# Two latent heads scored in one step of the even layer's attention, and a third tile behind its projections

## Chip, cores and metric

The kernel runs on 1 core of one Trainium2 chip. The metric is the device time of one execution in microseconds (us). The median of the runs of a kernel is what is compared.

## What is computed

A two-layer block runs first (feed-forward, a mixer of three branches, cross attention, feed-forward), then a second two-layer block on two streams of 256 rows each, x and a context. The change lies in layer 0 of that second block, its "even" mixer, which has four differential heads and four latent heads. For the latent heads (`mla_attend` in the reference) the part that matters is

```python
def mla_attend(qn, qr, kn, kr, v):
    s = (jnp.einsum('bhqd,bhkd->bhqk', qn, kn) + jnp.einsum('bhqd,bkd->bhqk', qr, kr)) * ((MLA_NOPE + MLA_ROPE) ** -0.5)
    p = softmax_f32(s)
    return jnp.einsum('bhqk,bhkd->bhqd', p.astype(v.dtype), v)
```

`qn`, `kn` have 128 numbers a head, `qr`, `kr` have 64; `kr` is shared by the heads. A differential head takes two softmaxes over keys of 64 numbers each and subtracts them. The context attends to its own 256 keys, x to 512 keys (the context's and its own). Everything is float32; the large weight products are split in three products of a faster type, the attention's products are plain float32.

## The kernel before

One Python program is run five times, once for each engine, and only that engine's instructions are emitted. Waits are counted semaphores, so the order on each engine is the order in which the program emits.

**Two streams woven by hand.** `second` starts two generators, `rows` (stream x) and `context`, and `weave` (L420) interleaves them. Each `yield` hands back an estimate in us of the TensorE work just emitted: about 2.8 for a block of weights of 256 x 512, 1.39 and 2.09 for the blocks of the two small projections out of the latent, 1.8 for a group of the modulation, 0 or a negative number where a stream has to wait for a latency. Rows go first, and the context goes first once it has earned 2.7 us (0.6 of what rows emitted). A stream that yields 0 or less is passed over until other work has been emitted. Where neither can go, `weave` emits a group of the modulation (`co.mods`, eight small products on a plain 512 KB block of `mod_w`). After each turn `tick` (L347) advances all jobs in flight by one step.

**Projections.** `Even` (L2258) has `latent_gemm`, `dv_gemm`, `dk_gemm`, `dq_gemm` and, for c = 0 and 1, `kv_gemm` and `q_gemm`. All but `dv_gemm` copy their result out of the banks into a tile `etk` taken from a ring (`Turns`, L679) and spawn a job: squares, sums, a power on GpSimd, the scaling (`group_norm`, L2182), for x also the rotation (`rope`, L2231), then the transposes into `kv` or `q` (`t32`, `two_halves`), and only then `turns.give`. `when_free` (L449) holds back the last block of the next projection while the next tile of the ring is taken. The ring has two tiles. A job needs some five ticks for the context and five to nine for x. `Even.ready` lets attention start when the last job is done. The context's feed-forward also stops after 16 blocks until x's projections are ready.

**Attention.** `Even.attend` (L2438) goes over 16 items (t, h), two tiles of 128 rows by eight heads; h < 4 are the differential heads, h >= 4 the latent heads. In step i it emits: the products with the values for item i - 3, the transposes of the probabilities of item i - 2 and their copy on ScalarE, then the scores of item i (one bank for each softmax), the maximum on VectorE and the exponential on ScalarE, and for a differential item i - 1 the combination of its two softmaxes. Then it yields 0, and `hops` turns that into a pause of 4 for x and of 0 for the context, so that at least one block of the other stream (2.8 us, in the context's attention sometimes a half block of 1.4) lies between two steps. The score products of a differential head take the rows 0 to 63 and 64 to 127 of the operands, one after the other; those of a latent head are one over 128 rows (L2507) and one over 64 rows (L2509), where even heads use rows 0 to 63 and odd heads rows 64 to 127.

**Banks.** `next_bank` hands out the PSUM bank of eight that was used longest ago; `hold` keeps a bank until `let_go`.

**Weights.** A ring of five raw slots is filled by SyncE in the order of use, three blocks ahead (`stage`, L465). ScalarE rounds a block (`whi`) and VectorE forms the rest (`wlo`). A slot is loaded again when both are done, or, for a plain block of the modulation, when TensorE has used it.

Of the kernel before, what the change touches and what calls it, by code (L numbers as in the profile page):

```python
# [13 lines left out]
P = 128  # L14
# [282 lines left out]
def next_bank(co, hold=False):  # L297

    b = min((b for b in co.banks if not b.held), key=lambda b: b.since)
    co.bi += 1  # L300
    b.held, b.since = hold, co.bi
    return b


def let_go(co, b):
    co.bi += 1
    b.held, b.since = False, co.bi
# [1071 lines left out]
def columns_of(co, dst, banks, tok, scale, *after):  # L1379
    a, b = (v.ap.rearrange("p (k n) -> p k n", k=2) for v in banks)  # L1380
    co.ac.wait_ge(tok, after)
    banks[0].drained = co.ac.activation(dst[:, 0:2, :], a, ACT.Copy, scale=scale).then_inc(co.s_ac)
    co.dv.wait_ge(tok, after)
    banks[1].drained = co.dv.tensor_scalar(dst[:, 2:4, :], b, scale, None, ALU.mult).then_inc(co.s_dv)
    return (banks[0].drained, banks[1].drained)
# [545 lines left out]
class Memory:  # L1931
# [13 lines left out]
    def keys(self):  # L1945
        def evac(banks, tok):
            self.dep["k"] = columns_of(self.co, self.k, banks, tok, 1.0, self.fe)
        return gemm_t(self.co, (self.mh, self.ml), self.mdep, self.co.A["xa_wkv"][self.l], 0, 512, evac)
# [309 lines left out]
class Even:  # L2258
# [179 lines left out]
    def attend(self, s, room, pr, at_, sm, mx, fe, done):  # L2438


        co, dep, lam = self.co, self.dep, self.co.lam
        dqt, qnt, qrt = self.q
        nk = 512 if s == 0 else 256
        ns = nk // P
        streams = (1, 0) if s == 0 else (1,)
        y = room.tile
        keys = lambda r, at: self.kv[r, 0:len(streams), at:at + 256]
        have = lambda names, ss: tuple(v for k, v in dep.items() if isinstance(k, tuple) and k[0] in names and k[1] in ss)
        kdep, qdep = have(("dk", "dv", "kn", "kr", "mv"), streams), have(("dq", "qn", "qr"), (s,))
        R = len(pr)  # L2450
        pfree, afree, smfree = [fe] * R, [fe] * 2, [fe] * R
        items = [(t, h) for t in range(2) for h in range(8)]
        n = len(items)
        yb, st, norms = {}, {}, []

        def normed_heads(t, b, a):
            done.append((yield from group_norm(co, [b], y, [(0, 4, P)], a, (t,))))

        for i in range(n + 3):
            if i >= 3:  # L2460
                t, h = items[i - 3]
                q = (i - 1) % 2
                if h % 4 == 0:
                    yb[h // 4] = next_bank(co, hold=True)
                b = yb[h // 4]
                v = [(self.dv if h < 4 else self.mv)[r][:, i, :] for r in streams for i in range(2)]
                hh = h % 4
                co.pe.wait_ge(st[i - 3], b.drained)
                for k in range(ns):
                    m = co.pe.matmul(b.ap[:, hh * P:(hh + 1) * P], at_[q][:, k, :], v[k][:, hh * P:(hh + 1) * P], start=k == 0, stop=k == ns - 1, skip_group_check=True).then_inc(co.s_pe, k == ns - 1)  # L2470
                afree[q] = m
                if h == 3:
                    co.ac.wait_ge(m, room.free)
                    a = co.ac.activation(y[:, t, 0:512], b.ap, ACT.Copy).then_inc(co.s_ac)
                    norms.append(normed_heads(t, b, a))
                if h == 7:
                    co.dv.wait_ge(m)
                    a = co.dv.reciprocal(sm[:, t, :], sm[:, t, :]).then_inc(co.s_dv)
                    co.dv.wait_ge(a, room.free)
                    b.drained = a = co.dv.tensor_tensor(y[:, t, 512:1024].rearrange("p (g n) -> p g n", n=P), b.ap.rearrange("p (g n) -> p g n", n=P), sm[:, t, :].unsqueeze(2).to_broadcast([P, 4, P]), ALU.mult).then_inc(co.s_dv)  # L2480
                    let_go(co, b)
                    done.append(a)
            if 2 <= i < n + 2:
                r, q = (i - 2) % R, i % 2
                p, es = pr[r], st[i - 2]
                b = next_bank(co)
                co.pe.wait_ge(es, b.drained)
                for k in range(ns):
                    m = co.pe.transpose(b.ap[:, k * P:(k + 1) * P], p[:, 0, k * P:(k + 1) * P], ident(co, p[:, 0, k * P:(k + 1) * P])).then_inc(co.s_pe, k == ns - 1)
                pfree[r] = m  # L2490
                smfree[r] = (m, es)
                co.ac.wait_ge(m, afree[q])
                b.drained = co.ac.activation(at_[q][:, 0:ns, :], b.ap[:, 0:nk].rearrange("p (k n) -> p k n", n=P), ACT.Copy).then_inc(co.s_ac)
                st[i - 2] = b.drained
            if i < n:
                t, h = items[i]
                ts_ = slice(t * P, (t + 1) * P)
                r = i % R
                p, es, scores = pr[r], [], []
                sc = 64 ** -0.5 if h < 4 else 192 ** -0.5  # L2500
                for j in range(2 if h < 4 else 1):
                    b = next_bank(co)
                    co.pe.wait_ge(kdep, qdep, b.drained)
                    if h < 4:
                        m = co.pe.matmul(b.ap[:, 0:nk], dqt[64 * j:64 * j + 64, h, ts_], keys(slice(64 * j, 64 * j + 64), 256 * h), skip_group_check=True, start=True, stop=True).then_inc(co.s_pe)
                    else:
                        co.pe.matmul(b.ap[:, 0:nk], qnt[:, h - 4, ts_], keys(slice(0, P), 1024 + 256 * (h - 4)), stop=False, skip_group_check=True, start=True)  # L2507
                        rr = slice(64 * (h % 2), 64 * (h % 2) + 64)
                        m = co.pe.matmul(b.ap[:, 0:nk], qrt[rr, (h - 4) // 2, ts_], keys(rr, 4096), start=False, skip_group_check=True, stop=True).then_inc(co.s_pe)  # L2509
                    scores.append((b, m))  # L2510
                for j, (b, m) in enumerate(scores):
                    co.dv.wait_ge(m, smfree[r])
                    a = co.dv.tensor_reduce(mx[:, r, j:j + 1], b.ap[:, 0:nk], AX, ALU.max).then_inc(co.s_dv)
                    co.dv.wait_ge(a)
                    a = co.dv.tensor_scalar(mx[:, r, j:j + 1], mx[:, r, j:j + 1], -sc, None, ALU.mult).then_inc(co.s_dv)
                    acc = sm[:, t, h - 4:h - 3] if h >= 4 else mx[:, r, 2 + j:3 + j]
                    co.ac.wait_ge(a, pfree[r])
                    b.drained = co.ac.activation(p[:, j, 0:nk], b.ap[:, 0:nk], ACT.Exp, scale=sc, bias=mx[:, r, j:j + 1], accum_out=acc).then_inc(co.s_ac)
                    es.append(b.drained)
                st[i] = tuple(es)  # L2520
            if 1 <= i < n + 1 and items[i - 1][1] < 4:
                r = (i - 1) % R
                p = pr[r]
                co.dv.wait_ge(st[i - 1])
                a = co.dv.reciprocal(mx[:, r, 2:4], mx[:, r, 2:4]).then_inc(co.s_dv)
                co.dv.wait_ge(a, co.gains)
                a = co.dv.tensor_scalar(mx[:, r, 3:4], mx[:, r, 3:4], lam[:, 2:3], None, ALU.mult).then_inc(co.s_dv)
                b = co.dv.tensor_scalar(p[:, 0, 0:nk], p[:, 0, 0:nk], mx[:, r, 2:3], None, ALU.mult).then_inc(co.s_dv)
                co.dv.wait_ge(a, b)
                st[i - 1] = co.dv.scalar_tensor_tensor(p[:, 0, 0:nk], p[:, 1, 0:nk], mx[:, r, 3:4], p[:, 0, 0:nk], ALU.mult, ALU.add).then_inc(co.s_dv)  # L2530
            norms = [g for g in norms if next(g, StopIteration) is not StopIteration]
            yield 0
        while norms:
            norms = [g for g in norms if next(g, StopIteration) is not StopIteration]
            yield 0
# [358 lines left out]
def second(co, start):  # L2894
    A = co.A
    at = lambda off, name, shape, dt=F32: place(co, start + 1024 * off, name, shape, dt)
# [4 lines left out]
    for a, b in zip(co.ch, old):  # L2901
# [4 lines left out]
    co.stream = {1: Stream(tile, [ready, ready], small(C_SM, C_SM + 4, 2), counts(co))}  # L2906
    co.sm, co.mx = small(C_SM + 4, C_SM + 12, 2), small(C_SM + 12, C_SM + 28, 4)
    co.smo, co.mxo = small(C_SM + 28, C_SM + 60, 2), small(C_SM + 60, C_SM + 68, 4)
    ev = Even(co, at(16, "kv", [P, 2, 4352]), at(50, "q", [P, 2560]), [at(60 + 4 * i, "etk", [P, 2, 512]) for i in range(2)],
              (at(68, "cqh", [P, 2, 256], F32R), at(70, "cql", [P, 2, 256], F32R)),  # L2910
              (at(72, "ckh", [P, 1, 256], F32R), at(73, "ckl", [P, 1, 256], F32R)),
              at(74, "ew", [P, 2, 512]), co.lb[:, :].rearrange("p (t n) -> p t n", t=2))
# [94 lines left out]
```

## Time and profile before

| | |
|---|---|
| median of 3 runs | 2571.64 us (2565.17 to 2572.57) |
| the profiled execution | 2567.47 us, span 2565.7 us |
| TensorE busy | 2487.4 us, 97% of the span |
| VectorE, ScalarE busy | 1661.2 us (65%), 1275.6 us (50%) |
| the second block | from about 1290 us to the end |
| context's projections and attention | about 1321 to 1464 us, and 1466 to 1538 us |
| x's projections and attention | about 1586 to 1699 us, and 1700 to 1822 us |

Engines are PE (TensorE), PEld (its weight loads, which overlap), DVE (VectorE), ACT (ScalarE), POOL (GpSimd), SP (SyncE). A line such as L175 is that of a helper, so the tile names tell which operation it is: `kv,q` are scores, `cst,pc` and `cst,px` the transposes of the context's and x's probabilities, `kv,atc` and `kv,atx` the products with the values, `cst,etk` the transposes of the projections, `raw,cst` the modulation.

### The profile page before, as it was taken

How to read it: one execution, taken by the hardware profiler on the slowest of the kernel's cores; microseconds unless marked ns; L12 is line 12 of the kernel's file. 1: busy time of each engine (PE TensorE's matmuls, PEld its weight loads, DVE VectorE, ACT ScalarE, POOL GpSimd, SP SyncE). 2: the span in 40 equal slices, each digit the busy share in tenths (PEclk: the TensorE clock that was granted, in tenths of full speed). 3: DMA queues.
4: the chain of work that ended last, by engine and by line, in shares of the span. 5: the costliest groups of instructions: out<-in, count | busy, mean ns of one | idle time of the engine just before them, and what ended most of it. 6: DMA issues, size and time to landing. Idle time of an engine off the chain costs nothing. (4 is left out here: it accounts for less than half of the span.)

```text
span 2565.7 us, 40494 instructions
## 1 busy us (share of the span) xinstructions
PE 2487.4 (97%) x16401; PEld 2151.3 (84%) x16401; DVE 1661.2 (65%) x2442; ACT 1275.6 (50%) x1844; POOL 197.0 (8%) x260
## 2 busy tenths in 40 slices
PE   8999999999999999999999998999999999998999
PEld 8998877889989988788888886878897887665998
DVE  5556785775576576867765767776655655766555
ACT  4445545544444445444454564655453544554543
POOL 1000000011021000001010201200000001100000
PEclk9999999999999999999999999999999999999999
DMA  8755565768577564557566535553556558635564
GB/s 276 251 180 161 145 190 178 255 203 298 158 220 247 164 206 129 172 166 259 193 193 183 165 99 177 160 173 99 164 177 226 197 189 220 193 114 195 166 192 137
DMA packets 239371, 479.14 MB, mean 187 GB/s; under 512 B 17584, under 2 KB 38328, under 8 KB 239120
## 3 DMA queue, kind: packets, MB, share of 16 engines
q1 hardware_dynamic: 222288, 421.19, 52.0%
q0 software_dynamic: 16896, 55.37, 6.8%
q8 instruction: 129, 2.11, 0.3%
q14 instruction: 58, 0.48, 0.1%
HBM read 475.33 MB, written 6.92 MB: 188 GB/s over the span
## 5 line engine op out<-in xcount | busy, mean ns | idle before, releaser
L126 DVE TENSOR_TENSOR wlo<-raw,whi 128x1024 fp32r<-128x1024 f32 (+3 forms) x786 | 912.9, 1173 | 661.3 <-ACT whi L167 660.0
L167 ACT ACTIVATE whi<-raw 128x1024 fp32r<-128x1024 f32 (+3 forms) x786 | 789.3, 1017 | 609.6 <-PE bank L175 516.4
L175 PE MATMUL bank<-xh,whi 128*128 128x256 f32 x2208 | 627.9, 284 | 3.6 <-DVE xl L126 2.5
L175 PE MATMUL bank<-xl,whi 128*128 128x256 f32 x2208 | 621.4, 281 | 0.0
L175 PE MATMUL bank<-xh,wlo 128*128 128x256 f32 x2208 | 621.3, 281 | 0.0
L175 PEld LDWEIGHTS bank<-xh,whi 128*128 128x128 f32 x2208 | 417.9, 189 | 16.3 <-issue 8.7
L175 PEld LDWEIGHTS bank<-xl,whi 128*128 128x128 f32 x2208 | 417.9, 189 | 1.2 <-issue 0.5
L175 PEld LDWEIGHTS bank<-xh,wlo 128*128 128x128 f32 x2208 | 417.7, 189 | 0.0
L175 PE MATMUL bank<-whi,xh 128*128 128x512 f32 (+2 forms) x632 | 256.7, 406 | 8.8 <-DVE xl L126 3.8
L175 PE MATMUL bank<-whi,xl 128*128 128x512 f32 (+2 forms) x632 | 247.8, 392 | 0.0
L175 PE MATMUL bank<-wlo,xh 128*128 128x512 f32 (+2 forms) x632 | 247.1, 391 | 0.0
L175 PE MATMUL bank<-whi,uh 128*128 128x512 f32 x528 | 211.1, 400 | 0.2 <-DVE ul L126 0.2
L175 PE MATMUL bank<-wlo,uh 128*128 128x512 f32 x528 | 209.4, 397 | 0.0
L175 PE MATMUL bank<-whi,ul 128*128 128x512 f32 x528 | 209.2, 396 | 0.0
L175 PEld LDWEIGHTS bank<-whi,xh 128*128 128x128 f32 x632 | 120.3, 190 | 48.0 <-DVE wlo L126 15.1
L175 PEld LDWEIGHTS bank<-whi,xl 128*128 128x128 f32 x632 | 119.9, 190 | 27.1
L175 PEld LDWEIGHTS bank<-wlo,xh 128*128 128x128 f32 x632 | 120.4, 191 | 25.5 <-issue 1.4
L126 POOL TENSOR_TENSOR cst<-cst 128x8 f32<-128x8 f32 (+4 forms) x50 | 74.9, 1511 | 679.0 <-DVE cst L133 679.0
L175 PEld LDWEIGHTS bank<-whi,uh 128*128 128x128 f32 x528 | 99.7, 189 | 24.5 <-issue 1.4
L175 PEld LDWEIGHTS bank<-whi,ul 128*128 128x128 f32 x528 | 99.5, 188 | 24.1
L175 PEld LDWEIGHTS bank<-wlo,uh 128*128 128x128 f32 x528 | 99.6, 189 | 22.5
L175 PE MATMUL bank<-x2h,whi 128*128 128x256 f32 x352 | 100.4, 285 | 1.4 <-DVE wlo L126 1.4
(440 smaller groups left out, 3752.5 us busy)
## 6 DMA issues: line engine op xcount, KB each, us to landing
raw<-in_ffn_w_in SPq DMA_DIRECT2D x280, 512.0 KB, 4.4
raw<-in_ffn_w_out SPq DMA_DIRECT2D x154, 512.0 KB, 4.7
raw<-in_w_mix_in SPq DMA_DIRECT2D x112, 512.0 KB, 3.6
raw<-in_mod_w SPq DMA_DIRECT2D x50, 512.0 KB, 4.3
store<-in_mod_w POOLq DMA_DIRECT2D x46, 512.0 KB, 8.1
raw<-in_od_w_in SPq DMA_DIRECT2D x40, 512.0 KB, 4.7
raw<-in_ffn_w_in SPq DMA_DIRECT2D x56, 256.0 KB, 2.8
raw<-in_w_branch SPq DMA_DIRECT2D x24, 512.0 KB, 3.4
```

The lines of the kernel that those rows point to most:

```text
L126: return Made(self.e and self.e.tensor_tensor(out, a, b, op))
L167: return Made(self.e and self.e.activation(out, a, f, **k))
L175: return Made(self.e and self.e.matmul(out, lhs, rhs, **k))
```

## The change

In `attend` the scores of a latent head are no longer emitted in its own step. At an even latent head two banks are held and four products are emitted: the two over 128 rows of this head and the next, then the two over 64 rows, one on rows 0 to 63 and the other on rows 64 to 127. The step of the odd head emits no scores; its maximum and exponential are emitted there as before, on the bank that waited. Each bank is let go after its exponential. And the ring of `etk` gets a third tile, placed at an offset of 94 KB beside the two at 60 and 64 KB.

```diff
-                for j in range(2 if h < 4 else 1):
-                    b = next_bank(co)
-                    co.pe.wait_ge(kdep, qdep, b.drained)
-                    if h < 4:
+                if h < 4:
+                    for j in range(2):
+                        b = next_bank(co)
+                        co.pe.wait_ge(kdep, qdep, b.drained)
                         m = co.pe.matmul(b.ap[:, 0:nk], dqt[64 * j:64 * j + 64, h, ts_], keys(slice(64 * j, 64 * j + 64), 256 * h), skip_group_check=True, start=True, stop=True).then_inc(co.s_pe)
-                    else:
-                        co.pe.matmul(b.ap[:, 0:nk], qnt[:, h - 4, ts_], keys(slice(0, P), 1024 + 256 * (h - 4)), stop=False, skip_group_check=True, start=True)
-                        rr = slice(64 * (h % 2), 64 * (h % 2) + 64)
+                        scores.append((b, m))
+                elif h % 2 == 0:
+                    two = [next_bank(co, hold=True) for _ in range(2)]
+                    for j, b in enumerate(two):
+                        co.pe.wait_ge(kdep, qdep, b.drained)
+                        co.pe.matmul(b.ap[:, 0:nk], qnt[:, h - 4 + j, ts_], keys(slice(0, P), 1024 + 256 * (h - 4 + j)), stop=False, skip_group_check=True, start=True)
+                    both = []
+                    for j, b in enumerate(two):
+                        rr = slice(64 * j, 64 * j + 64)
                         m = co.pe.matmul(b.ap[:, 0:nk], qrt[rr, (h - 4) // 2, ts_], keys(rr, 4096), start=False, skip_group_check=True, stop=True).then_inc(co.s_pe)
-                    scores.append((b, m))
+                        both.append((b, m))
+                    scores.append(both[0])
+                else:
+                    scores.append(both[1])
...
                     es.append(b.drained)
+                    if h >= 4:
+                        let_go(co, b)
...
-    ev = Even(co, at(16, "kv", [P, 2, 4352]), at(50, "q", [P, 2560]), [at(60 + 4 * i, "etk", [P, 2, 512]) for i in range(2)],
+    ev = Even(co, at(16, "kv", [P, 2, 4352]), at(50, "q", [P, 2560]), [at(o, "etk", [P, 2, 512]) for o in (60, 64, 94)],
```

## Rows read from the trace of the kernel before

**Rows 1.** The page: busy time of the engines, TensorE's granted clock in 40 slices
```profile
PE 2487.4 (97%) x16401; PEld 2151.3 (84%) x16401; DVE 1661.2 (65%) x2442; ACT 1275.6 (50%) x1844; POOL 197.0 (8%) x260
...
PEclk9999999999999999999999999999999999999999
```
**Rows 2.** Stretches, all engines: the two attentions, and 30 us later on
```profile
core 0: us, PE busy (x) PEld busy (x) DVE busy (x) ACT busy (x) POOL busy (x), PEclk, DMA share, GB/s
1466.00:1545.00 79.00, 75.40 (x510) 62.49 (x510) 52.69 (x122) 46.15 (x99) 2.01 (x2) 1.00 0.37 112
1700.00:1822.00 122.00, 120.25 (x754) 95.04 (x753) 76.93 (x133) 66.79 (x108) 2.04 (x2) 1.00 0.39 122
1955.00:1985.00 30.00, 24.79 (x163) 19.80 (x162) 15.29 (x19) 11.22 (x14) 1.38 (x2) 0.91 0.66 238
```
**Rows 3.** Timeline, x's attention, a latent head (start us, length us, instruction)
```profile
1742.38 0.30 PEld L175 LDWEIGHTS bank<-kv,q 128*128 128x128 f32 x2
1743.44 0.30 PEld L175 LDWEIGHTS bank<-kv,q 64*128 64x128 f32 x2 [0.76 <-issue]
1744.50 0.19 PEld L175 LDWEIGHTS bank<-ch,whi 128*128 128x128 f32 x1 [0.76 <-issue]
```
**Rows 4.** The same, a differential head and what follows it
```profile
1755.13 1.13 PE L175 MATMUL bank<-kv,q 64*128 64x512 f32 x4
1756.19 0.39 PE L175 MATMUL bank<-ch,whi 128*128 128x256 f32 x1
```
**Rows 5.** Timeline, context's attention: a differential head, a latent head, each with its follower
```profile
1466.60 0.70 PE L175 MATMUL bank<-kv,q 64*128 64x256 f32 x4
1467.23 0.50 PE L175 MATMUL bank<-whi,uh 128*128 128x512 f32 x1
...
1483.56 1.22 PE L175 MATMUL bank<-kv,q 128*128 128x256 f32 x4
1484.71 0.39 PE L175 MATMUL bank<-xh,whi 128*128 128x256 f32 x1
```
**Rows 6.** Timeline, from x's transposes to the next products with the values
```profile
1748.33 0.60 PE L178 MATMUL bank<-cst,px 128*128 128x128 f32 x4
1748.96 0.60 ACT L167 ACTIVATE atx<-bank 128x512 f32<-128x512 f32 x1 [1.21 <-PE bank L178]
...
1753.71 1.05 PE L175 MATMUL bank<-kv,atx 128*128 128x128 f32 x8
```
**Rows 7.** Timeline of PE around two turns of the ring, with DVE before the wait
```profile
1432.39 1.04 PE L178 MATMUL bank<-cst,etk 128*128 128x128 f32 x8
1433.18 0.42 PE L175 MATMUL bank<-whi,cqh 128*128 128x384 f32 x1
...
1440.14 1.28 DVE L126 TENSOR_TENSOR sa<-bank,sa 128x512 f32<-128x512 f32 x2
1441.52 1.30 DVE L126 TENSOR_TENSOR ul<-sa,uh 128x512 fp32r<-128x512 f32 x2
...
1444.40 1.00 DVE L132 TENSOR_SCALAR etk<-etk,cst 128x192 f32<-128x192 f32 x4
1445.45 0.66 PE L178 MATMUL bank<-cst,etk 128*128 128x128 f32 x4 [2.46 <-DVE etk L132]
```
**Rows 8.** Timeline of PE, context's attention, half blocks between the steps
```profile
1511.21 0.44 PE L178 MATMUL bank<-cst,pc 128*128 128x128 f32 x2 [1.57 <-DVE pc L136]
1515.38 0.44 PE L178 MATMUL bank<-cst,pc 128*128 128x128 f32 x2 [1.02 <-DVE pc L136]
1518.77 0.44 PE L178 MATMUL bank<-cst,pc 128*128 128x128 f32 x2 [0.27 <-DVE pc L136]
```
**Rows 9.** Timeline of PE, x's projections: a modulation group as filler, and a turn
```profile
1638.44 0.64 PE L175 MATMUL bank<-raw,cst 128*32 128x256 f32 x8
...
1658.43 1.03 PE L178 MATMUL bank<-cst,etk 128*128 128x128 f32 x8
1659.22 0.42 PE L175 MATMUL bank<-whi,cqh 128*128 128x384 f32 x1
```
**Rows 10.** Waits in total (engine, line, waited for), 1955 to 1985 us
```profile
ACT whi L167 <- DMA raw<-in_ffn_w_out: 9.2, 4, 5.5
PE bank L178 <- ACT modr L167: 5.2, 1, 5.2
```

## The prediction

> **What bounds the kernel now.** I read the page first. TensorE is busy for 2487.4 of 2565.7 us, at nearly full clock (2.4 GHz) throughout; no other engine is above 65% [rows 1]. So the kernel ends when TensorE has done its work plus what it waits, 78 us in all, and only two things can help: less work on TensorE, or fewer of its waits. Second I read the stretches in which the changed code runs. In x's attention TensorE is busy for 120.25 of 122 us, in the context's for 75.40 of 79 us, while VectorE is at 63 to 67% and ScalarE at 55 to 58% [rows 2]. There a microsecond of TensorE work saved is one off the end, as long as nothing new makes it wait. Third I read the timeline of TensorE for the few waits there are and for what they wait for.
>
> **Part 1, the pairing.** What does a product over 64 rows cost? In x's attention the first weight load of a latent head starts at 1742.38, that of its 64-row product at 1743.44, and the next block's at 1744.50 [rows 3]. So each of the two products takes 1.06 us, though the second uses half the rows. A differential head, which has two 64-row products on the two halves of the rows, takes 1756.19 - 1755.13 = 1.06 us for both [rows 4]. Two such products on different halves thus run at the same time. The change puts the 64-row products of two latent heads in exactly this order, on two banks, so a pair goes from 4 x 1.06 to 3 x 1.06 us. There are two row tiles and two pairs in each, so x gains 4 x 1.06 = 4.2 us.
>
> For the context a latent head takes 1484.71 - 1483.56 = 1.15 us, a differential one 1467.23 - 1466.60 = 0.63 us [rows 5]. Half of 1.15 is 0.58 for a product; a pair goes from 2.30 to 2 x 0.58 + 0.63 = 1.79, and the four pairs gain 4 x 0.5 to 4 x 0.58 = 2.0 to 2.3 us. I take 2.2. **Sum of part 1: -6.4 us**, nearly all on the path by [rows 2]. Its bounds: 0 if the products after a 128-row one did not overlap, and -6.8 if the context's gained 0.63 each; I take the value of the differential heads, since their products have the same shape, rows and bank use. The number of instructions stays the same.
>
> Here the Trainium skill gives another size. Its page "TensorE: Matmul & The Clock Gate", section "Part 3: Packing small matmuls — row/col tiling", reports 3.07 times for four row tiles. If two tiles kept the same share, 1.54 times, part 1 would be about -4.5 us, an estimate. The trace does not agree for this shape, and the measurement decides.
>
> The order of waits also changes. (a) At the even head the maximum of the first head now waits for one more 128-row product, 1.06 us later for x and 0.58 for the context; behind it on VectorE stand the maximum's scaling and the next `wlo`, on ScalarE the exponential and the next `whi`. Each block is used by TensorE only after one or two others, so I cost this at 0; uncovered it would be 4 x 1.06 + 4 x 0.58 = 6.6 us. (b) In the odd head's step no scores stand between the transposes and the next products with the values; only the other stream's block does. From transposes to the end of the copy it takes 1749.56 - 1748.33 = 1.23 us, and the block and scores cover it up to 1753.71 [rows 6]. Without scores 2.8 us of block remain, over twice what is needed: 0. Against a half block of 1.4 us it would be tight. (c) Two banks are held instead of one used; a latent pair still uses fewer banks in two steps than two differential heads, and no row of TensorE there waits for a bank: 0.
>
> Against (b) speaks a rule of the Trainium skill, "TensorEngine Tiling (Array Packing)", section "PSUM Bottleneck": tiling speeds TensorE up and not the emptying of PSUM, which may then bound it. With ScalarE and VectorE below 67% [rows 2] I do not see it here.
>
> **Part 2, the third tile.** It removes no instruction. It lets a projection's last block go where it stood behind the job that held its tile. The trace shows these turns: the context's first `q_gemm` starts at 1433.18, right behind the transposes at 1432.39 that freed the tile [rows 7], and x's at 1659.22 behind those at 1658.43 [rows 9]. TensorE was not idle at such a turn; it did the other stream's blocks. So the earlier start is worth nothing by itself, and what counts is which waits the new order has. I walked `weave`, with the ticks that each job needs in the order before. For the context `q_gemm(0)` goes one turn earlier and the last `q_gemm` two; its attention begins two blocks (5.6 us) earlier. For x all four go earlier and attention begins some three to four of the context's blocks earlier.
>
> - The wait of 2.46 us at 1445.45 arises because the scaling at 1444.40 stands on VectorE behind 2.6 us of the feed-forward's `sa` and `ul` [rows 7]. In the new order the scaling is emitted one turn before these, and a full block of 2.8 us lies before the transposes. It goes: -2.5 (bounds 0 and -2.5).
> - Three waits in the context's attention, 1.57 + 1.02 + 0.27 = 2.86 us, fall where half blocks (eight in a row) stand between steps while differential items are transposed [rows 8]. Two steps earlier, only the last two differential items meet half blocks, and the second has the longer score step of a pair before it. Some 1.4 remain: -1.5 (bounds 0 and -2.9). The case (b) above now falls on half blocks: 1.4 us against 1.23 needed, with nothing to spare. I leave it in the range as +0.5 to +1.
> - x's projections were twice at a point where neither stream could go, and a group of the modulation was emitted; 1638.44 is one of them [rows 9]. With a third tile neither point exists, so two groups come later. They land where the context's second normalisation needs the modulation finished, around 1955 to 1985 us. There weights already limit: the clock is granted at 0.91, TensorE busy for 24.8 of 30 us [rows 2], ScalarE waits 9.2 us for a load and TensorE 5.2 us for the modulation's copy behind it [rows 10]. A group needs 512 KB, at the 238 GB/s of that stretch [rows 2] 2.2 us, and gives TensorE 0.64 us of work [rows 9]. Between 0 (groups moved elsewhere) and 2 x 1.6 = 3.1 us; I take +1.5.
>
> **Sum of part 2: -2.5.** **Total: -8.9 us.** The profiled execution took 2567.5 us, so it would give 2558.6. The median shown is 2571.6, 4.2 higher; from it I get 2562.7, and predict **2563 us**.
>
> **The rivals.**
> 1. *Forecast*, 2559 to 2566 us: chance 0.42.
> 2. *Only the pairing counts.* The waits removed in part 2 come back at another place, as such waits follow from coincidences of the order, and the two groups cost their 1.5: 2571.6 - 6.4 + 1.5 = 2566.7. For it: nothing holds TensorE free at the new places. Chance 0.25.
> 3. *The stall at 1982 goes too.* The modulation's copy then no longer meets the late load: 5.2 us [rows 10], and the clock of 0.91 over 30 us [rows 2] back, 2.7 us: 2562.7 - 7.9 = 2554.8. Against it: the loads are as many as before. Chance 0.13.
> 4. *A new stall of that size* elsewhere: 2562.7 + 7.9 = 2570.6. Chance 0.10.
> 5. *The change does not do what it says*: no overlap behind 128-row products, so part 1 is 0: 2571.6 - 2.5 = 2569.1. Against it stand the differential heads [rows 4]. Chance 0.05.
> 6. *Slower: the odd step runs out of cover.* With the scores gone, TensorE waits for the copy of the transposes by all that it lost: 4 x 2.12 + 4 x 1.15 = 13.1 us, while part 1 gives 6.4. With the groups' 1.5: 2571.6 + 8.2 = 2579.8. This decides from the point where transposes to copied takes longer than a block, 2.8 us, for x; it takes 1.23 [rows 6]. Chance 0.05.
>
> **How the numbers follow.** A measurement of this kernel can tell about 0.3% (7.7 us) from no change: faster is below 2563.9, slower above 2579.3. Most but not all of 1 (0.30), all of 3 (0.13) and a little of 2 (0.05) are faster: 0.48. Case 6 and a bad form of 4 are slower: 0.07. The rest, 0.45, is no difference. The likeliest case alone spans 2559 to 2566. For 8 in 10 the range takes in rivals 2 to 5, down to 2554 and up to 2572.
>
> **What would show it.** Right: in both attentions a latent pair is followed by its block after about 3.2 us (x) and 1.8 us (context), and the steps of odd heads have no `kv,q`; the wait of 2.46 us at the projections is gone, and `raw,cst` no longer appears between x's projections; TensorE's busy time in the second block falls by some 6 us. Wrong: a wait of `kv,atx` or `kv,atc` for ScalarE's copy in odd steps (case b), a score product that waits for a bank (case c), a longer wait than 5.2 us for `modr`, or a fall in the clock at a place where it was full. The prediction fails as a whole if waits after 1840 us, which the change touches only through the order, move by more than 6 us.

## The result and the profile after

The changed kernel takes 2547.9 us (median of 4 runs, 2546.7 to 2549.3) against 2570.4 for the kernel before on the same chip: ratio 0.9919, interval 0.9906 to 0.9931, or 20.8 us less (18 to 24); the two medians themselves differ by 22.4. Gains in us below are such ratios times the median of the kernel before. Two more sets of runs gave 0.9932 (0.9920 to 0.9943) and 0.9922 (0.9908 to 0.9935). The forecast was 8.9 us less, and 2547.9 lies below its range of 2554 to 2572. The profiled execution went from 2565.7 to 2545.8 us of span.

The page of the kernel after, which answers to [rows 1]:

```profile
PE 2475.8 (97%) x16401; PEld 2147.7 (84%) x16401; DVE 1658.8 (65%) x2442; ACT 1272.9 (50%) x1842; POOL 195.3 (8%) x260
```

TensorE works 11.6 us less and waits 8.3 us less (2565.7 - 2487.4 = 78.3 against 2545.8 - 2475.8 = 70.0). Where? I cut both executions at the same instructions: first `cst,cy`, last use of `coh`, last `x2h`, first `okt`, last `raw,cst`, end. I call the five stretches the context's, x's, the next one, the odd layer's attention and the rest. Nothing was edited in the last three. The stretches of the kernel before, then of the kernel after (from:to, length, then busy time of each engine; TensorE's clock near the end of the line):

```profile
1297.10:1583.90 286.80, 274.91 (x1685) 236.96 (x1686) 185.28 (x336) 153.16 (x249) 28.78 (x21) 0.99 0.52 156
1583.90:2133.70 549.80, 537.80 (x3572) 463.61 (x3571) 350.35 (x544) 282.19 (x404) 38.21 (x31) 0.99 0.54 177
2133.70:2227.10 93.40, 86.41 (x381) 66.82 (x379) 61.51 (x71) 46.36 (x60) 19.72 (x19) 0.98 0.79 222
2227.10:2347.90 120.80, 111.65 (x841) 75.41 (x840) 75.30 (x157) 69.61 (x152) 6.47 (x4) 0.97 0.43 138
2347.90:2565.70 217.80, 204.83 (x1392) 188.62 (x1384) 128.10 (x144) 92.46 (x110) 3.70 (x5) 0.98 0.54 170
```
```profile
1295.50:1577.90 282.40, 271.97 (x1684) 236.62 (x1685) 184.42 (x336) 153.26 (x249) 26.92 (x21) 0.99 0.51 158
1577.90:2116.90 539.00, 530.56 (x3564) 461.28 (x3563) 349.18 (x545) 280.70 (x403) 39.34 (x31) 1.00 0.55 180
2116.90:2210.30 93.40, 85.65 (x381) 67.00 (x379) 61.59 (x71) 45.28 (x59) 19.72 (x19) 0.98 0.77 219
2210.30:2327.70 117.40, 110.87 (x845) 74.76 (x848) 74.49 (x157) 68.50 (x151) 6.47 (x4) 0.99 0.44 142
2327.70:2545.80 218.10, 205.44 (x1392) 189.12 (x1384) 128.83 (x144) 93.43 (x111) 3.70 (x5) 0.97 0.54 172
```

The context's stretch gained 4.4 us, x's 10.8, and the odd layer's attention, in which nothing was edited, 3.4. Length less busy time is TensorE's waiting: 11.9 to 10.4, 12.0 to 8.4, and 9.15 to 6.5 us. These are single executions, and the same program varies: the kernel before and four of those below run the same instructions up to 1590 us, and their context's stretch took 286.8 to 291.5 us, with 10.9 to 13.4 us of waits. A difference of 2 or 3 us between two profiles shows little by itself. How much of the work was the pairing's? The same stretches for the products of `kv` alone (the number after the length: TensorE), before, then after:

```profile
1297.10:1583.90 286.80, 25.23 (x128) 15.65 (x128) 1.51 (x3) 4.94 (x9) 0.99 0.52 156
1583.90:2133.70 549.80, 42.51 (x192) 23.16 (x192) 1.51 (x3) 4.61 (x9) 0.99 0.54 177
```
```profile
1295.50:1577.90 282.40, 22.37 (x128) 15.07 (x128) 1.51 (x3) 4.97 (x9) 0.99 0.51 158
1577.90:2116.90 539.00, 37.64 (x192) 22.37 (x192) 1.51 (x3) 4.63 (x9) 1.00 0.55 180
```

2.9 us for the context and 4.9 for x, 7.7 in all. So the 19.9 us of span are 7.7 of paired products, 8.3 of waits, and 3.9 of TensorE's other work, which did the same instructions in less time: the clock was granted at 0.995 in the mean against 0.993, and 0.001 of 2550 us is 2.6 us, an estimate that covers the 3.9.

One pair of each kind after, for [rows 3] and [rows 5]: weight loads of a pair of x with the next block's, the same pair on TensorE, then a pair of the context with its follower on TensorE. The fence in between is the latent head of [rows 3] on TensorE, in the kernel before.

```profile
1719.59 0.30 PEld L175 LDWEIGHTS bank<-kv,q 128*128 128x128 f32 x2
...
1721.50 0.30 PEld L175 LDWEIGHTS bank<-kv,q 64*128 64x128 f32 x4 [0.76 <-issue]
1722.56 0.19 PEld L175 LDWEIGHTS bank<-whi,xh 128*128 128x128 f32 x1 [0.76 <-DVE wlo L126]
```
```profile
1719.69 2.94 PE L175 MATMUL bank<-kv,q 128*128 128x512 f32 x8
1722.56 0.50 PE L175 MATMUL bank<-whi,xh 128*128 128x512 f32 x1
```
```profile
1742.49 2.08 PE L175 MATMUL bank<-kv,q 128*128 128x512 f32 x4
1744.50 0.39 PE L175 MATMUL bank<-ch,whi 128*128 128x256 f32 x1
```
```profile
1510.73 1.66 PE L175 MATMUL bank<-kv,q 128*128 128x256 f32 x8
1512.32 0.39 PE L175 MATMUL bank<-xh,whi 128*128 128x256 f32 x1
```

Both 64-row products of x together take 1.06 us, so the overlap is whole. The two 128-row products before them take 1.91, not 2 x 1.06: less than when a 64-row product follows each. By its weight loads a pair of x takes 2.97 us in place of 2 x 2.12. The first load of a step starts 0.10 to 0.11 us ahead of its product, though, so by the starts on TensorE it is 1722.56 - 1719.69 = 2.87 in place of 2 x 2.01. One of the context takes 1.59 in place of 2 x 1.15.

The single starts behind these merged rows show why two 128-row products cost less. Each product is two records. The second record of a 128-row product is followed after 0.43 us by another 128-row product and after 0.52 us by a 64-row one. In the context it is 0.22 and 0.31. So a change in the number of rows cost 0.09 us here, and a pair in the new order has fewer of them. By these starts a pair of x gains 1.15 us: 1.05 of a 64-row product that now runs beside the other, and 0.09 of a change that is gone. By busy time it is 4.9 / 4 = 1.2.

The waits of TensorE up to x's projections, before, then after (total, times, longest). `y` are rows that are being normalised. Not shown are 2.0 us for `cy` in the kernel before; they were 0.3 in another execution of the same instructions.

```profile
PE bank L178 <- DVE pc L136: 3.6, 4, 1.6
PE bank L178 <- DVE etk L132: 3.5, 2, 2.5
PE bank L175 <- DVE wlo L126: 3.2, 2, 2.7
PE bank L178 <- DVE y L132: 1.8, 2, 1.3
```
```profile
PE bank L178 <- DVE etk L132: 3.5, 3, 1.8
PE bank L178 <- DVE y L132: 3.4, 2, 2.9
PE bank L178 <- DVE pc L136: 1.6, 1, 1.6
PE bank L175 <- DVE wlo L126: 1.2, 2, 0.6
PE bank L175 <- ACT atc L167: 1.1, 2, 0.8
```

The wait of 2.46 us for `etk` [rows 7] is gone from its place, and two others have come, before and after it:

```profile
1439.07 0.66 PE L178 MATMUL bank<-cst,etk 128*128 128x128 f32 x4 [0.55 <-DVE etk L132]
1452.92 0.66 PE L178 MATMUL bank<-cst,etk 128*128 128x128 f32 x4 [1.85 <-DVE etk L132]
```

At 1982 us, where TensorE waited 5.2 us for `modr` [rows 10], it now waits 2.7 us for `wlo`, at 1979. (`modr` is the tile into which ScalarE copies a result of the modulation; `wlo` is VectorE's part of a split block of weights.)

The walk of the order in the prediction held. From the start of its stretch to its first score product, the context takes 164.0 us in place of 169.5 (5.6 less foretold), and x 104.6 in place of 116.5 (three to four blocks of 2.8 us foretold). No `raw,cst` stands between 1582 and 1886 us, so the two groups did leave x's projections.

### The profile page after: what moved, and what is told of

It reads as the page before. It is cut to its first block and busy times, and to the rows that moved or that the text cites. A ratio compares the mean times of both kernels' runs of the same rounds, so it can differ in the third digit from the quotient of the medians.

```text
span 2545.8 us, 40493 instructions
## 1 busy us (share of the span) xinstructions
PE 2475.8 (97%) x16401; PEld 2147.7 (84%) x16401; DVE 1658.8 (65%) x2442; ACT 1272.9 (50%) x1842; POOL 195.3 (8%) x260
## 5 line engine op out<-in xcount | busy, mean ns | idle before, releaser
L126 DVE TENSOR_TENSOR wlo<-raw,whi 128x1024 fp32r<-128x1024 f32 (+4 forms) x786 | 912.4, 1172 | 669.0 <-ACT whi L167 667.5
L167 ACT ACTIVATE whi<-raw 128x1024 fp32r<-128x1024 f32 (+4 forms) x786 | 789.2, 1017 | 623.6 <-PE bank L175 514.6
L175 PE MATMUL bank<-ch,whi 128*128 128x256 f32 x352 | 101.1, 287 | 0.0
```

What stands on the lines that cost most here:

```text
L126: return Made(self.e and self.e.tensor_tensor(out, a, b, op))
L167: return Made(self.e and self.e.activation(out, a, f, **k))
L175: return Made(self.e and self.e.matmul(out, lhs, rhs, **k))
```

## The experiments

**The two parts, apart and together.** First the pairing alone (the diff without its last hunk), and the third tile alone (only its last hunk).

> The kernel before with the pairing alone, two tiles. The order of all jobs, blocks and modulation groups stays that of before. Theory A (the sum on record): 6.4 us faster than before, ratio 0.9975. Theory B (read off the two traces: the score products of the two attentions took 7.7 us less of TensorE's time, and the rest of the gain came with the third tile): 7 to 8 us faster, 0.9970, the wait of 2.46 us for `etk` and the stall of 5.2 us for `modr` still there. Theory C (the gain is one of coincidence, and each part alone gives little): under 3 us. If the pairing shifts later work against its loads, the stall for `modr` changes although the order does not.

> The kernel before with the third tile alone, heads one by one. The order of jobs is that of the kernel after. Theory A (on record): 2.5 us faster, 0.9990. Theory B (the trace after has no stall for `modr` and no fall of the clock there, and fewer waits in the odd layer's attention): 11 to 14 us faster, 0.9950. Theory C (the stall went because the pairing moved the work against the loads): at most 3 us faster, with a stall of 4 us or more left around 1980 us.

> The kernel after once more, as the common measure of this set. Additive parts: its gain is the sum of the two parts alone, 20.8 us, ratio 0.9919. If the parts interact, it is more than 2 us off their sum.

Measured against the kernel before: pairing alone 0.9980 (0.9972 to 0.9989), 5.1 us less; third tile alone 0.9956 (0.9944 to 0.9968), 11.3 us less; both 0.9932, 17.5 us less. The parts add up within their intervals, and the larger one is the third tile, which the sum on record held for the smaller. The products of `kv` took 7.7 us less with the pairing alone and as long as before with the tile alone. The tile alone took TensorE's waits of x's stretch from 12.0 to 7.2 us and those of the odd layer's attention from 9.15 to 6.6. The pairing alone kept the stall for `modr` (5.4 us). Its gain of 5.1 us (2.8 to 7.2) is smaller than 7.7. Its one profile has 3 us more of waits in the context's stretch: 1.2 for `atc`, which belong to the pairing, and 1.6 more for `y`, which don't, as a kernel with this stretch unedited has the same 3.4 us for `y`. So 1.2 us of the difference are accounted for, and the rest is within the interval.

**The overlap alone.** In the kernel after, each 64-row product behind its own 128-row one:

```diff
                     two = [next_bank(co, hold=True) for _ in range(2)]
+                    both = []
                     for j, b in enumerate(two):
                         co.pe.wait_ge(kdep, qdep, b.drained)
                         co.pe.matmul(... qnt ...)
-                    both = []
-                    for j, b in enumerate(two):
                         rr = slice(64 * j, 64 * j + 64)
                         m = co.pe.matmul(... qrt ...)
```

> The kernel after, but within a pair each 64-row product follows its own 128-row product, so that the two 64-row products can't run at the same time; banks, order of jobs and the steps stay. Theory A: it loses the overlap alone, 6.4 us (4 x 1.06 for x, 4 x 0.55 for the context), and the waits stay as in the kernel after. Rival: pairing itself changed the waits (scores of two heads in one step), and with these gone too the loss is another: under 4 us if the odd step's lack of scores costs waits that the longer step hides, over 8 us if the waits removed came from the pairing.

Measured: 0.9966 (0.9954 to 0.9978), so the overlap is worth 17.5 - 8.7 = 8.8 us beside the third tile, give or take some 4 us by the two intervals. The products of `kv` are back at the time of before:

```profile
1295.20:1580.30 285.10, 25.35 (x128) 15.71 (x128) 1.51 (x3) 4.97 (x9) 0.99 0.51 157
1580.30:2125.80 545.50, 42.62 (x192) 23.20 (x192) 1.51 (x3) 4.63 (x9) 1.00 0.54 178
```

That is 8.0 us more than in the kernel after, the whole of the 8.8 within noise. So the work saved is the overlap and not the mere place of the scores.

And the 1.1 us of waits for `atc` are gone with the overlap. In the kernel after they stand in the steps of odd heads on half blocks; ScalarE there has a table load and the feed-forward's `sa` ahead of the copy of the transposes:

```profile
1519.94 0.61 ACT L167 ACTIVATE whi<-raw 128x512 fp32r<-128x512 f32 x1
1520.57 1.28 ACT L167 ACT_TABLE_LOAD   x1
1521.87 0.60 ACT L167 ACTIVATE sa<-bank 128x512 f32<-128x512 f32 x1
1522.36 0.38 ACT L167 ACTIVATE atc<-bank 128x256 f32<-128x256 f32 x1
```
```profile
1522.79 0.71 PE L175 MATMUL bank<-kv,atc 128*128 128x128 f32 x4 [0.80 <-ACT atc L167]
```

So there TensorE saves 0.7 us by a pair and waits 0.8 us for ScalarE. The missing scores alone don't make this wait: the kernel without the overlap has none in its odd steps either, and no wait for `atc`. It differs in that a pair takes TensorE 0.7 us longer there. Which of ScalarE's operations would have to move to keep the 0.7 was not tried.

**Which stream needs the third tile.** A ring of three for one stream, of two for the other, heads one by one:

```diff
-        self.turns = Turns(co, tks, None)
+        self.tks = tks
+        self.turns = Turns(co, tks[:2], None)
...
+    ev.turns = Turns(co, ev.tks, None)
     ev.start(counts(co))
```

> The kernel before with the third tile for x's projections alone; the context has two. The modulation's groups and the blocks of the tail then stand as in the kernel after. The third tile alone gained 11 us for both. Theory A (most of it comes from the tail, where the modulation's groups meet other blocks): 7 to 9 us faster than before; no wait of over 4.5 us near 1980 us, and the odd layer's attention with some 6.6 us of waits in place of 9.2. Theory B (the context's earlier start is worth the larger part, as the sum on record has it with 4.0 us against -1.5 for x): at most 4 us faster.

> The kernel before with the third tile for the context's projections alone; x has two, so both groups of the modulation stay in x's projections and the tail keeps the order of before. Theory A: 2 to 3 us faster than before, with 5.2 us for `modr` near 1982 still there. Theory B (the sum on record): 4 us faster, since the wait of 2.46 us at the projections and 1.5 us of those in the context's attention go. The parts for x and for the context should add up to the 11 us of both.

Measured: for x alone 0.9973 (0.9964 to 0.9982), 6.9 us less; for the context alone 0.9982 (0.9973 to 0.9991), 4.6 us less. Together 11.5, as the tile for both gave (11.3). The first lies near theory A. The second has an interval of 2.3 to 6.9 us and can't tell its two theories apart. With it for the context alone the stall for `modr` stayed (4.4 us), and the odd layer's attention kept its 9.2 us of waits. With it for x alone those were 6.6, and 4.5 us for `wlo` stood in place of the stall.

**Why the stall at 1982 went.** ScalarE ahead of the stall in the kernel before, which answers to the 9.2 us of [rows 10]:

```profile
1976.62 1.06 ACT L167 ACTIVATE whi<-raw 128x1024 fp32r<-128x1024 f32 x1 [5.51 <-DMA raw<-in_ffn_w_out]
1977.93 1.06 ACT L167 ACTIVATE whi<-raw 128x1024 fp32r<-128x1024 f32 x1 [0.26 <-DMA raw<-in_ffn_w_out]
1980.85 1.06 ACT L167 ACTIVATE whi<-raw 128x1024 fp32r<-128x1024 f32 x1 [1.86 <-DMA raw<-in_ffn_w_out]
1981.81 0.37 ACT L167 ACTIVATE modr<-bank 128x256 f32<-128x256 f32 x1
```

The modulation's last group had started at 1976.4 and took 0.6 us, and its copy stood behind three splits that waited for loads. I tried three edits: the transposes of `modr` one turn later in the kernel before; its two filler groups in x's projections left out; and the two groups put back in the kernel after.

```diff
     let_go(co, bank)
     yield
+    if (l, blk) == (1, 1):
+        yield
     b = next_bank(co, hold=True)
```
```diff
-            took = next(co.mods, None)
+            took = next(co.mods, None) if turn not in (118, 139) else 1.8
```
```diff
     while not a.over:
+        turn += 1
+        if turn in (118, 137):
+            next(co.mods, None)
```

> The kernel before with the transposes of `modr` near 1982 us one turn later, behind a block (one more group of the modulation enters the burst by this). Theory A (the stall is ScalarE's copy standing behind a split whose load is late): the wait for `modr` is gone and what remains, for `wlo`, is under 1.5 us: 4 to 8 us faster than before. Theory B (the loads of the burst are late for TensorE anyway): a wait for `wlo` of 3 to 5 us takes its place, and the gain is under 3 us.

> The kernel before without the two groups of the modulation in x's projections (the turns are left empty, so the other jobs keep their order); they come later, and the burst ahead of the context's second normalisation has seven groups in place of four. Theory A (their move removes the stall): 5 to 8 us faster than before, no wait of over 3 us near 1982. Theory B (late loads): the stall stays or grows, to 5 to 9 us, and the kernel is 0 to 5 us slower than before. The sum on record took +1.5 us for this move.

> The kernel after, with two groups of the modulation put back to about the turns at which the kernel before has them, in x's projections and ahead of x's attention; every other job keeps its place among blocks, so the burst of groups ahead of the context's second normalisation has three groups in place of six. In question is why the wait of 5.2 us for `modr` near 1982 us became one of 1.5 to 4.4 us for `wlo`. Theory A (the two groups moved did it, since the end of a block of the modulation falls elsewhere): the stall for `modr` returns, 4 to 7 us slower than the kernel after. Theory B (late weight loads did it, and the third tile only changed which work meets them): fewer groups in the burst, so the wait near 1980 is under 2 us, the clock stays at its upper level there, and the kernel is 0 to 4 us faster than the one after.

Transposes later: 0.9994 (0.9985 to 1.0004), no clear gain, though at the place it went as theory A has it:

```profile
1979.83 0.50 PE L175 MATMUL bank<-whi,uh 128*128 128x512 f32 x1 [1.42 <-DVE wlo L126]
1983.08 0.44 PE L178 MATMUL bank<-cst,modr 128*128 128x128 f32 x2 [0.20 <-ACT modr L167]
```

Waits in x's stretch fell from 12.0 to 8.4 us, and 1.4 came back in the next one. Groups later: 0.9990 (0.9980 to 0.9999), 2.6 us less, with 1.8 us for `wlo` and 1.2 for `modr` left of the 5.2. That is the direction of theory A at a third to half of its size; a longer burst did not make the stall longer, as theory B had it. Groups early: 0.9916 (0.9898 to 0.9934), 0.9 us for `modr` left, and the kernel no slower than the one after. So neither theory holds whole. In all three, an order in which the copy isn't right behind the late splits is rid of most of the 5.2 us, and what is left is 0.9 to 3.0 us, for `modr` and for late loads. But a stall that goes is not a gain of its size. The first edit aimed at it alone, and gained 1.5 us with 0 inside its interval. In the four profiles with two tiles for x and none of these three edits the stall measured 4.4 to 5.4 us.

**The clock behind a wait.** The repeats of the kernel after and of the one with early groups:

> The kernel after again, beside the next one: ratio to before 0.992 to 0.993, median near 2549 us. The wait for `wlo` near 1979 us was 2.7 us in one execution, with the clock at its upper level behind it, and 4.1 us in another, with the lower level behind it; here one of the two again.

> The kernel after with two groups of the modulation back in x's projections, again. It had 0.9 us of waits near 1980 us where the kernel after has 2.7 to 4.1 us. Theory B (late loads in the burst): 1.8 to 3.2 us faster than the kernel after, or up to 5 us with the fall of the clock that it avoids. Rival (the gain is given back where loads are dense in the second feed-forward and the odd layer): within 1 us.

Measured 0.9922 and 0.9912 (0.9898 to 0.9926), medians 2549.5 and 2546.3. Four profiled executions have the order of the kernel after up to this place. Their wait for `wlo` was 1.5, 2.7, 4.1 and 4.6 us, and x's stretch 537.6, 539.0, 541.4 and 542.5 us long: from the shortest to the longest it grew by 4.9 us, 3.1 of them waiting at this place. TensorE's busy time grew by 1.5 us, from 530.6 to 532.1, and that is the clock. From the product behind the wait to the transposes of `modr` twelve products run. In two of these executions, with the windows around them (clock third from the end):

```profile
1979.03 0.50 PE L175 MATMUL bank<-whi,uh 128*128 128x512 f32 x1 [2.71 <-DVE wlo L126]
...
1981.93 0.38 PE L178 MATMUL bank<-cst,modr 128*128 128x128 f32 x2
...
1979.00:1982.00 3.00, 2.97 (x13) 2.38 (x14) 1.23 (x1) 1.36 (x3) 0.00 (x0) 1.00 1.01 378
```
```profile
1978.77 0.80 PE L175 MATMUL bank<-whi,uh 128*128 128x512 f32 x1 [4.12 <-DVE wlo L126]
...
1984.06 0.63 PE L178 MATMUL bank<-cst,modr 128*128 128x128 f32 x2
...
1978.77:1984.06 5.29, 5.29 (x13) 4.02 (x13) 2.45 (x2) 3.43 (x4) 0.00 (x0) 0.50 0.52 194
```

The same twelve products took 2.90 us at the upper level (granted 1.00, 2.4 GHz) and 5.29 at the lower one (0.50, 1.2 GHz). In the execution with the wait of 4.6 us they took 4.40, with the last few back at the upper level; in the one with 1.5 us, 2.91.

**The odd layer's attention.** The modulation's last groups are given out in a burst there. A block of the modulation is eight groups, its "columns" in the expectations below. By the order in which the program emits, the burst begins with the fourth group of a block in the kernel before and with the third in the kernel after, one group fewer being done by then. The traces agree: 21 and 22 groups follow. These two kernels shift that count by one, by moving one group, and change nothing else:

```diff
-    for _ in range(n):
+    for k in range(n):
         yield
-        next(co.mods, None)
+        if k < n - 1:
+            next(co.mods, None)
```
```diff
+        if turn in (292,):
+            next(co.mods, None)
```

> The kernel before with one group of the modulation less in x's second feed-forward, so the last burst begins one group earlier in the modulation (its third column of block 3, as in the kernel after, in place of the fourth); one group more is done at the end. Theory A (the waits in the odd layer's attention hang on where the modulation's blocks end against the attention's steps): waits there fall from 9.2 to about 6.6 us, those for `ato` (1.9) and `modr` (1.0) go, and the kernel is 2 to 4 us faster than before. Rival (they hang on the moment at which the loads come, which the third tile shifted): the waits stay at 8.5 to 9.2, no change.

> The kernel after with one group of the modulation more, at a turn in x's second feed-forward's end, so that the last burst begins at the fourth column of block 3 as in the kernel before. Theory A: waits in the odd layer's attention rise from 6.5 to about 8.7 us, with those for `ato` and `modr` back; 2 to 4 us slower than the kernel after (ratio to before 0.993 to 0.994). Rival: unchanged, 0.992.

The first (one group fewer, in the kernel before): 0.9983 (0.9975 to 0.9992), 4.4 us less. The second (one more, in the kernel after): 0.9943 (0.9929 to 0.9957), 5.4 us slower than the kernel after at 0.9922. That comparison is across two sets of runs; with the kernel after at 0.9932 or 0.9919, as its other sets have it, it is 2.8 or 6.2. The first test has no such weakness. In its profile this stretch is 3.4 us shorter than before, so 1 of its 4.4 us (2.1 to 6.4) is not located. This stretch in both:

```profile
2232.50:2349.90 117.40, 110.87 (x845) 74.54 (x848) 74.52 (x157) 68.49 (x151) 6.48 (x4) 0.99 0.43 142
```
```profile
2214.10:2333.50 119.40, 110.20 (x837) 74.30 (x840) 75.22 (x157) 69.65 (x152) 6.47 (x4) 0.99 0.43 139
```

Its waits are 6.5 and 9.2 us, the very values of the kernels after and before, now swapped. What comes and goes is a wait of 1.9 us for `ato`, the transposed probabilities of this attention, and two of 0.5 for `modr`, as here in the kernel before:

```profile
2293.88 0.44 PE L178 MATMUL bank<-cst,modr 128*128 128x128 f32 x2 [0.50 <-ACT modr L167]
2312.44 0.44 PE L178 MATMUL bank<-cst,modr 128*128 128x128 f32 x2 [0.50 <-ACT modr L167]
...
2329.40 0.66 PE L175 MATMUL bank<-ato,ovx 128*64 128x128 f32 x8 [1.88 <-ACT ato L167]
```

All seventeen profiles sort by this count: a burst from the third group, 6.5 to 6.8 us of waits (ten profiles); from the fourth or fifth, 8.1 to 9.2 (seven).

**No burst at all.** Five groups evenly placed in x's projections and attention of the kernel after; and the same with the count put right.

> The kernel after with five groups of the modulation at evenly spaced turns of x's projections and attention, where the loads run at 106 to 132 GB/s; then no burst is left ahead of the context's second normalisation, one group stands among five blocks. Theory B (late loads in the burst): no wait near 1980, no fall of the clock there: 2 to 6 us faster than the kernel after, about 23 to 26 us faster than before. Rival (the waits return at the next place where loads are dense): no faster than the kernel after within 2 us.

> The kernel after with five groups evenly placed in x's projections and attention (no burst ahead of the context's second normalisation), and one less in x's second feed-forward, so that the last burst begins at the same group as in the kernel after. The same without the last correction had x's stretch at 537.1 us against 539.0 to 542.5 of the kernel after, but 8.7 us of waits in the odd layer's attention against 6.6. Theory A: waits there 6.6, median 2544 to 2547 us, ratio 0.990 to 0.9915, faster than the kernel after by 2 to 5 us. Rival (the burst-free order loses elsewhere too): ratio 0.992 or more.

The first: 0.9937 (0.9921 to 0.9952), no better than the kernel after. x's stretch had its fewest waits (6.4 us), but the count was that of the kernel before, and the odd layer's attention had 8.7. The second: 0.9915 (0.9902 to 0.9928), median 2545.1, 117.4 us in that stretch again. The two differ by the count alone, a third test of it: 5.6 us, across sets as well. It and the kernel with early groups have the lowest medians of the study, some 3 us below the kernel after, and can't be told from it: the intervals of the ratios overlap.

## Why the prediction was wrong, by its steps

**What bounds the kernel** held: TensorE's work and waits are the whole difference.

**Part 1, -6.4.** The mechanism was right, the term too small. The overlap is whole: two 64-row products take the 1.06 us of one. The figure of the Trainium skill from "TensorE: Matmul & The Clock Gate", section "Part 3: Packing small matmuls — row/col tiling", is for four row tiles; scaled to two it gave the estimate of -4.5, and that is not what two row tiles do here. The step that mis-sized the term is "from 4 x 1.06 to 3 x 1.06". It priced all products alike, and neighbouring 128-row products of x take 0.95 us each by their weight loads, as no change of rows stands between them. So a pair gains 1.2 us, not 1.06. In the context a 64-row product takes 0.63 us and not half of 1.15, so a pair gains 0.7, not 0.5 to 0.58. Busy time fell by 7.7, beyond the bound of -6.8; in time the pairing alone gave 5.1 (2.8 to 7.2). Case (b) came as "Against a half block of 1.4 us it would be tight": 1.1 us of waits for `atc`, put in the range at +0.5 to +1. Case (c) cost nothing: no wait for a bank stands in either attention. Case (a) cost nothing in x, where the waits for `px` fell from 1.7 to 0.8 us.

**Part 2, the context, -4.0.** The sum agrees (-4.6 measured, 2.3 to 6.9), by luck, as its terms don't. The wait of 2.46 us was priced at -2.5 and gave nothing: it came back as 0.55 and 1.85 us, and those for `etk` are 3.5 us in all before and after. Those for `pc` fell from 3.6 to 1.6, by 2.0 where I had 1.5, though three more executions of the same instructions had 2.6 with two tiles, so the drop may be 1.0. A wait I hadn't looked at, for `wlo`, fell from 3.2 to 1.2, and was 2.6 to 3.2 wherever the context has two tiles. Those for `y` (1.8 to 3.4) differ as much between executions of the same instructions and count for neither side.

**Part 2, x, +1.5.** This is the step that failed, and it is most of the miss: -6.9 was measured. I saw that two groups of the modulation leave x's projections, and priced them by their own work and loads where they land. But leaving them out alone gains 2.6 us (0.3 to 5.1) where +1.5 stood. That the modulation's copy then no longer stands right behind late splits is the likely reason and is not shown: moving the transposes alone gave no clear gain. And in the third tile's order one group fewer is done when the odd layer's burst begins, which by itself is worth 4.4 us (2.1 to 6.4); the prediction had nothing for that. 2.6 + 4.4 = 7.0 fits x's 6.9, but with such intervals, and with 4.5 us still waited for `wlo` in the profile of x's tile alone, this is a fit and not a proof. The third tile for x alone with the count put back would tell, and was not run. The emission order could have been walked to the end blind, as I did for the projections; it showed the count, though not its price.

**The sum as the runs have it:** 8.8 (pairing beside the third tile) + 4.6 + 6.9 = 20.3 us, against 17.5 to 20.8 measured for the whole. With the pairing alone, 5.1, in place of 8.8 it is 16.6.

**The rivals.** Rival 3 (the stall at 1982 goes too, 0.13) was nearest, and only half true: in place of 5.2 us for `modr` stand 1.5 to 4.6 for `wlo`, and the fall of the clock is avoided in some executions and paid in others. Its argument against, "the loads are as many as before", was true, but the order in which the splits and the copy stand changed with the loads unchanged. Rivals 2, 4, 5 and 6 fell: the waits did not come back, no new stall came, the overlap is there, and case (b) came at 1.1 us, not 13.1.

**What would make it wrong.** I had named waits after 1840 us moving by more than 6 us. They moved by 5.3 (35.9 to 30.5) between the two profiles, and by 4.9 and 3.7 in two more profiles of the kernel after, so the test did not even fire. It looked at waits alone and left out what the clock gives back with them, by the estimate above 2.6 us for each 0.001 of the mean.

## What to carry to other kernels

When an edit shifts a hand-woven order, the price of a moved filler is not its own work but what it stands beside at every later landing; count it to the end of the program. Test such a gain by shifting the count alone: a gain that a one-group shift in the unchanged kernel gives as well is luck of the order and not a merit of the edit. And look where a result's copy stands behind work that waits for loads: here TensorE waited 5.2 us for a copy of 0.37 us. Moving it takes the stall away at its place; whether the kernel gains has to be measured. Last, take a second profile before crediting a difference of 2 or 3 us.

## What the runs showed of the hardware

Three things I had not expected. By their weight loads two 128-row fp32 products in a row take 1.91 us, and a 128-row one with a 64-row one 2.12; a change in the number of rows between neighbours costs 0.09 us. A wait of 4.1 us was followed by a clock at the lower level and cost 2.4 us more than itself, one of 2.7 us was not; only these executions show it, and they set no limit between the two. And the same program waits 2.7, 4.1 or 4.6 us at one place from one execution to the next, with x's stretch 3.5 us longer for it, so one profile can't price a stall whose length hangs on loads.
